# Banded attention beside a memory projection: who splits the weights, and where the scores stand

## Chip, cores and metric
One core of a Trainium2 chip runs the whole program. The metric is the device time of one execution in microseconds (us). The engines are TensorE (PE; its weight loads are PEld), VectorE (DVE), ScalarE (ACT), GpSimd (POOL) and SyncE (SP), which issues most transfers.

## What is computed
One layer of a hybrid decoder for 1024 prompt tokens and 64 sample tokens, 1088 columns in all:

```
x += 0.5 * swiglu_1(norm(x))
h  = norm(x);  u, gate, q, k, v = h @ w_in
     lru_out  = norm(rg_lru(conv(u)) * gelu(gate))
     attn_out = norm(swa(rope(q), rope(k), v))        # blocks of 128 queries over 256 keys, masked to a band, with sinks
x += concat(lru_out, attn_out) @ w_out
mk, mv = norm(mem) @ w_ck, norm(mem) @ w_cv           # 256 memory tokens: the "memory projection"
x += cross_attend(norm(x), mk, mv)
x += 0.5 * swiglu_2(norm(x));  y = norm(x)
```

All values are fp32. Every large product is made of three TensorE products: a weight is split into a high part (rounded to the type fp32r) and a low part (the rest), the activations likewise, and hi*hi + hi*lo + lo*hi is summed.

## The kernel before
Activations lie feature-major, as `[128, tile, 1088]`. The columns are worked in three chunks `CH` of 288, 512 and 288. Each engine has a program of its own, written out by hand and ordered by semaphores.

**Plain projections** (`w_in`, `w_out`, `w_cq`, `w_co`). `plain` (L699) runs tiles of 128 output features, in turn in slot 0 (PSUM banks 0 to 2) and slot 1 (banks 3 to 5). `tile` (L690) has three chunks of 24 matmuls. For `mix` (before `w_in`) and `xattn` (before `w_cq`) the first two tiles run before the norm of their input is known, and `sum_squares` (L565) between tile 0 and tile 1 makes the three column sums of squares with a matmul by ones, into banks 6, 7 and 6 again; `sum_chunk` (L570) waits for VectorE's `mean_squares` (L1288) of the first sum before it writes bank 6 again. On VectorE `mean_squares` handles all three chunks; only then `inverse_rms` (L1297) makes the reciprocal chunk by chunk, and after each chunk `scaled_take` takes that chunk of tile 0 out of PSUM. Tile 2 on TensorE needs tile 0's chunks taken (`g_ev`).

**Banded attention with the memory projection in between.** There are NB = 8 blocks of 128 queries. In a block TensorE runs `block_step` (L822): `scores` of the next block, `turn_p` (transposes of the probabilities) for key head 0, `rotate` for the block after the next, `turn_p` for head 1, `memory_tile` 0, `weigh` 0, `memory_tile` 1, `weigh` 1, `turn_v` of the next block. A `memory_tile` is 24 matmuls of a memory projection, into one place in bank 7. In an even block (s = 0, a pair of `w_ck` tiles) tile 0 reads weight slot 0 and tile 1 slot 1; in an odd block (a pair of `w_cv` tiles) each reads both slots. Each slot has one buffer for the raw weights, one for the high parts and one for the low.

GpSimd splits each slot with `split_short` (L446) in four quarters of 128x256: a multiplication by ones gives the high part (L452), a subtraction the low one (L453). It starts as soon as `mem_mm` says that TensorE is done with the slot. SyncE loads the next raw tile when `w_split` says that the slot is split.

VectorE's `block_step` (L1646) of block b: `add_mask` for b+1 (L1587), `rope_read` (L1572, L1574), `maxima` (L1592 to L1595), `rope` for b+2 (L1579 to L1583), `stage_v`, `take_memory` for both tiles of b (PSUM to SBUF), `probabilities` of b+1 (L1601), `take_result` of b. ScalarE's `block_step` (L1127): two copies of the transposed probabilities (L1131), `exps` of b+1 (L1119, L1121), `take_v` of b+1 (L1125).

After block 6 the sample tokens are rotated, and their scores stand in block 7 between `memory_tile` 0 and `weigh` 0. Behind block 7 ScalarE issues four stores (L1154 to L1159), makes the sample group's exponentials (L1162), VectorE its probabilities (L1684), TensorE turns them (L886, L887) and weighs (L896, L897); then come the squares of the attention's norm (L1003) and the output projection.

Of the kernel before, what the change touches and what calls it, by code (L numbers as in the profile page):

```python
# [22 lines left out]
F32 = mybir.dt.float32  # L23
# [5 lines left out]
P = 128  # L29
# [84 lines left out]
def build(nc, t_in, t_out):  # L114
    ctx = ExitStack()
    with ctx:
        def sem(name):
            return ctx.enter_context(nc.semaphore(name))
# [181 lines left out]
        pt_mm, pt_ev = sem("pt_mm"), sem("pt_ev")  # L300
        v_st, vt_mm, vt_ev = sem("v_st"), sem("vt_mm"), sem("vt_ev")
        pv_mm, o_ev = sem("pv_mm"), sem("o_ev")
        mem_mm, kv_ev = sem("mem_mm"), sem("kv_ev")
        swa_own = sem("swa_own")
        mem_in = sem("mem_in")

# [132 lines left out]
        def _(pool):  # L439
# [45 lines left out]
            def split_plain(s, p):  # L485
                pool.wait_ge(w_in[s], (p + 1) * 16)
                split_short(w_raw[s], w_hi[s], w_lo[s], Steps(pool, w_pool, p * (2 * KT // SHORT) + s * (KT // SHORT)), w_split[s])
# [18 lines left out]
                    .then_inc(lru_normed, 1)  # L506


            for s in range(2):
                pool.wait_ge(mem_mm, 1 + s)  # L510
                split_plain(s, PAIR_KV + 1)
            with pool.Fori(1, NB // 2) as i:
                for s in range(2):
                    pool.wait_ge(mem_mm, i * 4)
                    split_plain(s, i * 2 + PAIR_KV)
                for s in range(2):
                    pool.wait_ge(mem_mm, i * 4 + (1 + s))
                    split_plain(s, i * 2 + (PAIR_KV + 1))
            for s in range(2):
                pool.wait_ge(mem_mm, 2 * NB)  # L520
                split_plain(s, PAIR_OUT)
# [24 lines left out]
        def _(pe):  # L546
# [20 lines left out]
            def sum_squares(key, chunks, adds, src=acc):  # L567

                for c in range(len(chunks)):
                    sum_chunk(key, chunks, c, adds, src)  # L570
# [121 lines left out]
            def tile(stage, p, s, n0, feed=None):  # L692

                pe.wait_ge(w_split[s], p + 1)
                for c, (o, n) in enumerate(CH):
                    pe.wait_ge(g_ev[stage], n0 + c + 1)
                    ins = product(ps[:, 3 * s + c, 0:n], w_hi[s], w_lo[s], c, feed)
                    ins.then_inc(w_mm[s], 1)

            def plain(stage, pair0, pairs, feed, norm=None):  # L700
                tile(stage, pair0, 0, 0, feed=feed)
                if norm:
                    sum_squares(norm, CH, 2 * KT)
                tile(stage, pair0, 1, NC)
                with pe.Fori(1, pairs) as i:
                    for s in range(2):
                        tile(stage, i + pair0, s, i * (2 * NC) + s * NC)
# [90 lines left out]
            def weigh(b, kv):  # L798

                pe.wait_ge(pt_ev, b * 2 + kv + 2)  # L800
                for half in range(2):
                    ins = pe.matmul(ps[kv * HD:(kv + 1) * HD, 6, :], v_n[half][:, kv * HD:(kv + 1) * HD],
                                    p_T[:, half, kv * GRP:(kv + 1) * GRP, :], start=(half == 0), stop=(half == 1))
                return ins
# [16 lines left out]

            def block_step(b, s, more=True, rot=True):  # L822

                if more:
                    scores(b + 1)
                pe.wait_ge(p_done, b + 1)
                turn_p(b, s, 0)
                if rot:
                    rotate(b + 2)
                turn_p(b, s, 1)  # L830
                pe.wait_ge(vt_ev, b + 1)
                if rot:
                    pe.wait_ge(rot_ev, b + 3)
                else:
                    pe.wait_ge(o_ev, b + 1)
                memory_tile(b, s, 0)
                if not more:
                    sample_scores()
                weigh(b, 0)
                memory_tile(b, s, 1)  # L840
                weigh(b, 1).then_inc(pv_mm, 1)
                if more:
                    turn_v(b + 1)

# [27 lines left out]
            rotate(1)  # L872
            pe.wait_ge(rot_ev, 2)
            turn_v(0)
            pe.wait_ge(memn_lo_done, 1)
            with pe.Fori(0, NB // 2 - 1) as i:
                block_step(i * 2, 0)
# [26 lines left out]


            pe.wait_ge(x_tab, 16)
            pe.wait_ge(g_ev["cq"], 6 + NC * KT)

            def x_scores(b):
# [82 lines left out]
        def _(act):  # L992
# [130 lines left out]
            def take_v(b, s):  # L1123
                act.wait_ge(vt_mm, b + 1)
                act.activation(v_n[s][:, :], ps[:, 7, WIN:2 * WIN], ACT.Copy).then_inc(vt_ev, 1)  # L1125

            def block_step(b, s, more=True):  # L1127
                for kv in range(KVH):

                    act.wait_ge(pt_mm, b * 2 + kv + 1)  # L1130
                    act.activation(p_T[:, :, kv * GRP:(kv + 1) * GRP, :], ps[:, 4:6, :], ACT.Copy)\  # L1131
                       .then_inc(pt_ev, 1)
                if more:
                    exps(b + 1, 1 - s)
                    take_v(b + 1, 1 - s)

            act.sem_inc(pt_ev, 1)
            exps(0, 0)
# [40 lines left out]
            for c in range(NC):  # L1179
                hi_parts("cat", cat_tile, "g_cat", lambda c: act.wait_ge(attn_normed, c + 1), [c], range(LT, KT))  # L1180
                if c < NC - 1:
                    hi_parts("cat", cat_tile, "g_cat", chunks=[c + 1], tiles=range(LT))
            act.dma_start(t_out["mem_k"], mem_kT[:, :, :]).then_inc(stored, 16)
            act.dma_start(t_out["mem_v"], mem_v[:, :, :]).then_inc(stored, 16)

# [86 lines left out]
        def _(dve):  # L1272
# [337 lines left out]

            ROPE_STEPS, SWA_STEPS = 1, 5

            def take_memory(b, s, j):

                dve.wait_ge(mem_mm, b * 2 + j + 1)
                if s == 0:
                    to = mem_kT[:, bass.ds(b + j, 1), :].squeeze(1)
                else:
                    to = mem_v[:, j, bass.ds(b * P - P, 2 * P)]
                take_out(to, ps[:, 7, 256:512]).then_inc(kv_ev, 1)  # L1620

            def take_result(b):
# [4 lines left out]
            def block_step(b, s, rot=True):  # L1627
                steps = Steps(dve, swa_own, b * (ROPE_STEPS + SWA_STEPS) + (2 * ROPE_STEPS + SWA_STEPS))
                add_mask(b + 1, 1 - s, masks[:, 2 - s, :])
                if rot:  # L1630
                    rope_read(b + 2)
                maxima(b + 1, 1 - s, steps)
                if rot:
                    rope(b + 2, s, steps)
                stage_v(b + 1)
                for j in range(2):
                    take_memory(b, s, j)
                probabilities(b + 1, 1 - s, steps)
                assert steps.n == SWA_STEPS + (ROPE_STEPS if rot else 0)
                take_result(b)  # L1640
# [26 lines left out]
                              q_r[:, :, 0:TS].rearrange("p g (b t) -> p g b t", b=NS),  # L1667
                              rot_q[:, :, 0:TS].rearrange("p g (b t) -> p g b t", b=NS), ALU.add)
            dve.tensor_tensor(ks_r[:, :], ks_r[:, :], rot_k[:, 0:TS], ALU.add).then_inc(s_rope, 1)
            take_memory(NB - 1, 1, 0)  # L1670
            own.done(dve.tensor_scalar(st8[:, 7, 0:4], c_("sink_s", 0, 4), HD ** 0.5, None, ALU.mult))
            dve.wait_ge(kvc_in, 48)
            dve.wait_ge(s_sc_mm, 1)
# [3 lines left out]
            own.done(dve.tensor_tensor(st8[:, 0, 0:4], st8[:, 0, 0:4], st8[:, 7, 0:4], ALU.max))  # L1677
            own.done(dve.tensor_scalar(st8[:, 1, 0:4], st8[:, 0, 0:4], -(HD ** -0.5), None, ALU.mult))
            dve.tensor_tensor(st8[:, 2, 0:4], st8[:, 1, 0:4], c_("sink_s", 0, 4), ALU.add).then_inc(s_nmax, 1)
            take_memory(NB - 1, 1, 1)  # L1680
            dve.wait_ge(s_exp, 1)
            own.done(dve.tensor_tensor(st8[:, 5, 0:4], st8[:, 3, 0:4], st8[:, 4, 0:4], ALU.add))
            own.done(dve.reciprocal(st8[:, 6, 0:4], st8[:, 5, 0:4]))
# [284 lines left out]
```

## Time and profile before

| | us |
|---|---|
| median of 3 runs | 2483.28 (2482.21 to 2483.57) |
| the profiled execution: its time | 2480.83 |
| its span | 2479.0 |
| PE busy / DVE / POOL / ACT busy in it | 2333.8 / 1431.7 / 1029.9 / 444.1 |
| mean granted TensorE clock | 0.973 of full speed |

The span is what the trace shows from the first to the last instruction; 1.8 us of the execution's time lie outside of it. Busy time of matmuls is modelled, so start times are the surer reading. In the rows below a timeline row has: start in us, length in us, engine, line, operation, written<-read, count, and in square brackets how long the engine had been idle and what ended that. "ACTq" is ScalarE's sequencer while it issues a transfer.

### The profile page before, as it was taken

The page shows a single profiled execution, that of the slowest core. Times are in us where ns is not written, and L with a number is a line of the kernel's source. Part 1 is how long each engine was busy: PE and PEld are TensorE (multiplying, and loading weights), DVE is VectorE, ACT ScalarE, POOL GpSimd, SP SyncE. Part 2 cuts the span into 40 slices and gives each one's busy share as a digit, 9 for nine tenths or more (in the row PEclk, how much of TensorE's full clock was granted, in tenths as well). Part 3 has the DMA queues.
Part 4 walks back from the last instruction along what each step waited for, and adds up shares of the span by engine and source line. Part 5 has one row for each costly group of instructions (what it writes and reads, how often), then busy time and mean ns, then how long its engine had stood idle before and what let it go on. Part 6 is the DMA issues. An engine that isn't in the chain of part 4 may idle for free.

```text
span 2479.0 us, 35690 instructions
## 1 busy us (share of the span) xinstructions
PE 2333.8 (94%) x13994; PEld 2070.5 (84%) x13994; DVE 1431.7 (58%) x1864; ACT 444.1 (18%) x908; POOL 1029.9 (42%) x717
## 2 busy tenths in 40 slices
PE   6999999999999999688789989999999999999997
PEld 5899998999998887556578977889998999999896
DVE  7755555655555775876454324447655655565564
ACT  5111100110110416233322013231000000000002
POOL 2543443434433164546635430344434434344333
PEclk9999999999999999899889999999999999999998
DMA  4111101111010010201211134011011110110102
GB/s 142 69 40 45 47 20 51 51 51 51 34 42 26 26 43 26 97 28 58 71 55 48 34 137 170 26 59 69 21 47 51 51 51 35 50 40 28 68 0 74
DMA packets 40285, 131.89 MB, mean 53 GB/s; under 512 B 5799, under 2 KB 11047, under 8 KB 37799
## 3 DMA queue, kind: packets, MB, share of 16 engines
q1 hardware_dynamic: 37280, 127.80, 14.8%
q10 hardware_dynamic: 2951, 3.35, 0.4%
q8 instruction: 36, 0.59, 0.1%
q14 instruction: 18, 0.15, 0.0%
HBM read 123.33 MB, written 7.81 MB: 53 GB/s over the span
## 4 chain that ended last, share of the span: by engine, by line
PE 85%; DVE 6%; POOL 5%; ACT 3%; issue 1%; DMA 1%; POOLq 0%; SPq 0%; DVEq 0%; ACTq 0%
PE ps L552 27%; PE ps L554 26%; PE ps L553 26%; POOL w_hi L452 2%; POOL w_lo L453 1%; PE ps L961 1%; PE ps L914 1%; DVE act_lo L1315 1%; DVE rstd L1302 1%; DVE mem_raw L1544 1%; PE ps L737 1%; PE ps L578 0%; ACT sq L1003 0%; DVE y L1825 0%; ACT act_hi L1018 0%
## 5 line engine op out<-in xcount | busy, mean ns | idle before, releaser
L552 PE MATMUL ps<-act_hi,w_hi 128*128 128x288 f32 (+1 forms) x1968 | 658.0, 334 | 48.0 <-DVE act_lo L1315 34.8
L553 PE MATMUL ps<-act_lo,w_hi 128*128 128x288 f32 (+1 forms) x1968 | 653.1, 332 | 0.0
L554 PE MATMUL ps<-act_hi,w_lo 128*128 128x288 f32 (+1 forms) x1968 | 652.6, 332 | 0.0
L552 PEld LDWEIGHTS ps<-act_hi,w_hi 128*128 128x128 f32 x1968 | 377.5, 192 | 81.9 <-issue 38.6
L553 PEld LDWEIGHTS ps<-act_lo,w_hi 128*128 128x128 f32 x1968 | 377.6, 192 | 29.6
L554 PEld LDWEIGHTS ps<-act_hi,w_lo 128*128 128x128 f32 x1968 | 377.0, 192 | 29.1
L452 POOL TENSOR_TENSOR w_hi<-w_raw,ones 128x256 fp32r<-128x256 f32 x216 | 193.9, 898 | 472.2 <-PE ps L554 440.0
L1358 DVE SCALAR_TENSOR_TENSOR x<-ps,x 128x288 f32<-128x288 f32 (+1 forms) x504 | 263.6, 533 | 188.0 <-PE ps L554 172.8
L552 PE MATMUL ps<-hid_hi,dn_hi 128*128 128x288 f32 (+1 forms) x1056 | 348.7, 330 | 3.6 <-issue 3.6
L554 PE MATMUL ps<-hid_hi,dn_lo 128*128 128x288 f32 (+1 forms) x1056 | 347.7, 329 | 0.0
L553 PE MATMUL ps<-hid_lo,dn_hi 128*128 128x288 f32 (+1 forms) x1056 | 347.7, 329 | 0.0
L552 PE MATMUL ps<-act_hi,up_hi 128*128 128x288 f32 (+1 forms) x1056 | 347.6, 329 | 0.0
L554 PE MATMUL ps<-act_hi,up_lo 128*128 128x288 f32 (+1 forms) x1056 | 347.5, 329 | 0.0
L553 PE MATMUL ps<-act_lo,up_hi 128*128 128x288 f32 (+1 forms) x1056 | 347.5, 329 | 0.0
L1351 DVE TENSOR_TENSOR hid_lo<-hid_t,hid_hi 128x288 fp32r<-128x288 f32 x132 | 329.7, 2549 | 0.4
L443 POOL TENSOR_TENSOR w_hi<-w_raw,ones 128x1024 fp32r<-128x1024 f32 x42 | 102.0, 2428 | 506.8 <-PE ps L554 490.6
L1326 DVE TENSOR_TENSOR gate_t<-ps,rstd 128x288 f32<-128x288 f32 x132 | 70.0, 532 | 375.7 <-PE ps L554 375.1
L443 POOL TENSOR_TENSOR dn_hi<-w_raw,ones 128x1024 fp32r<-128x1024 f32 x22 | 52.9, 2406 | 396.1 <-PE ps L554 325.2
L552 PEld LDWEIGHTS ps<-hid_hi,dn_hi 128*128 128x128 f32 x1056 | 199.9, 189 | 19.2 <-issue 4.0
L554 PEld LDWEIGHTS ps<-hid_hi,dn_lo 128*128 128x128 f32 x1056 | 199.7, 189 | 16.0
L553 PEld LDWEIGHTS ps<-hid_lo,dn_hi 128*128 128x128 f32 x1056 | 200.0, 189 | 15.3
L553 PEld LDWEIGHTS ps<-act_lo,up_hi 128*128 128x128 f32 x1056 | 198.5, 188 | 16.0
(244 smaller groups left out, 2934.3 us busy)
## 6 DMA issues: line engine op xcount, KB each, us to landing
w_raw<-in_w_ffn SPq DMA_DIRECT2D x66, 512.0 KB, 3.7
w_raw<-in_w_plain SPq DMA_DIRECT2D x54, 512.0 KB, 3.6
ff_raw_up<-in_w_ffn SPq DMA_DIRECT2D x44, 512.0 KB, 4.4
ff_raw_down<-in_w_ffn SPq DMA_DIRECT2D x22, 512.0 KB, 6.4
ck_T<-in_ck SPq DMA_DIRECT2D x8, 1024.0 KB, 7.7
cv_n<-in_cv SPq DMA_DIRECT2D x8, 1024.0 KB, 4.9
x<-in_x SPq DMA_DIRECT2D x2, 1152.0 KB, 11.0
x<-in_x SPq DMA_DIRECT2D x1, 2048.0 KB, 12.0
```

The lines of the kernel that those rows point to most:

```text
L443: steps.done(pool.tensor_tensor(hi[:, :, :], raw[:, :, :], one, ALU.mult))
L452: steps.done(pool.tensor_tensor(hi[:, r, :], raw[:, r, :], one, ALU.mult))
L453: ins = pool.tensor_tensor(lo[:, r, :], raw[:, r, :], hi[:, r, :].bitcast(F32), ALU.subtract)
L552: pe.matmul(out, wh, ah, start=(first and n == 0), stop=False)
L553: pe.matmul(out, wh, al, start=False, stop=False)
L554: ins = pe.matmul(out, wl, ah, start=False, stop=end)
L737: pe.matmul(ps[:, 6 + n_ % 2, 0:n], bd[:, ct, j // NC, :], mix[:, M_U + ct, o:o + n], start=True, stop=True).then_inc(lru_mm, 1)
L914: pe.matmul(ps[:, h // 2, (h % 2) * NM:(h % 2 + 1) * NM], xq_b[:, 2 * h + d, :], mem_kT[:, 2 * h + d, :], start=(d == 0), stop=(d == 1))
L961: ins = pe.matmul(ps[:, 6 + kt // 4, (kt % 4) * P:(kt % 4 + 1) * P], mem_v[:, mt, kt * P:(kt + 1) * P], xp_T[:, mt, kt // 2, :], start=(mt ...
L1326: dve.tensor_tensor(gate_t[:, o:o + n], ps[:, c, 0:n], rstd[:, o:o + n], ALU.mult)\
L1351: dve.tensor_tensor(hid_lo[s][:, o:o + n], hid_t[:, o:o + n], hid_hi[s][:, o:o + n].bitcast(F32), ALU.subtract).then_inc(f["hid_lo"], 1)
L1358: dve.scalar_tensor_tensor(out=x[:, m, o:o + n], in0=ps[:, DOWN_BANKS[n_ % 8], 0:n], scalar=0.5, in1=x[:, m, o:o + n], op0=ALU.mult, op1=A ...
```

## The change
1. **Scores.** `scores` no longer opens a TensorE block. `scores(1)` stands in front of the loop, and a block b with `rot` ends with `weigh` 1, `scores(b+2)`, `turn_v(b+1)`.
2. **High parts.** In the seven blocks 0 to 6 ScalarE copies each whole raw slot (128x1024) to its high part, behind `take_v`; it signals `kv_hi`. GpSimd only subtracts, four quarters a slot.
3. **Takes.** VectorE takes memory tile 0, now in front of `rope`; ScalarE takes memory tile 1, in front of `take_v`, and in block 7 in front of the four stores.
4. **Sums of squares.** In `plain` with a norm the third sum is made behind tile 1 and not in front of it.
5. Two waits on `kv_ev` are added in front of the users of the memory keys and values.

```diff
-            for s in range(2):
-                pool.wait_ge(mem_mm, 1 + s)
-                split_plain(s, PAIR_KV + 1)
-            with pool.Fori(1, NB // 2) as i:
-                for s in range(2):
-                    pool.wait_ge(mem_mm, i * 4)
-                    split_plain(s, i * 2 + PAIR_KV)
-                for s in range(2):
-                    pool.wait_ge(mem_mm, i * 4 + (1 + s))
-                    split_plain(s, i * 2 + (PAIR_KV + 1))
+            with pool.Fori(0, NB - 1) as b:
+                for s in range(2):
+                    pool.wait_ge(kv_hi, b * 2 + (s + 1))
+                    for k in range(0, KT, SHORT):
+                        r = slice(k, k + SHORT)
+                        ins = pool.tensor_tensor(w_lo[s][:, r, :], w_raw[s][:, r, :], w_hi[s][:, r, :].bitcast(F32),
+                                                 ALU.subtract)
+                    ins.then_inc(w_split[s], 1)
+            pool.sem_inc(w_pool, (NB - 1) * (2 * KT // SHORT))
...
                 if norm:
-                    sum_squares(norm, CH, 2 * KT)
+                    sum_squares(norm, CH[:2], 2 * KT)
                 tile(stage, pair0, 1, NC)
+                if norm:
+                    sum_chunk(norm, CH, 2, 2 * KT)
...
             def block_step(b, s, more=True, rot=True):
-                if more:
-                    scores(b + 1)
...
                 weigh(b, 1).then_inc(pv_mm, 1)
+                if rot:
+                    scores(b + 2)
                 if more:
                     turn_v(b + 1)
...
             turn_v(0)
+            scores(1)
...
+            def take_memory(b, s):
+                act.wait_ge(mem_mm, b * 2 + 2)
+                if s == 0:
+                    to = mem_kT[:, bass.ds(b + 1, 1), :].squeeze(1)
+                else:
+                    to = mem_v[:, 1, bass.ds(b * P - P, 2 * P)]
+                act.activation(to, ps[:, 7, 256:512], ACT.Copy).then_inc(kv_ev, 1)
...
                 if more:
                     exps(b + 1, 1 - s)
+                take_memory(b, s)
+                if more:
                     take_v(b + 1, 1 - s)
+                    for j in range(2):
+                        act.wait_ge(w_in[j], b * 16 + (PAIR_KV + 2) * 16)
+                        act.activation(w_hi[j], w_raw[j][:, :, :], ACT.Copy).then_inc(kv_hi, 1)
...
                 maxima(b + 1, 1 - s, steps)
+                take_memory(b, s)
                 if rot:
                     rope(b + 2, s, steps)
                 stage_v(b + 1)
-                for j in range(2):
-                    take_memory(b, s, j)
                 probabilities(b + 1, 1 - s, steps)
...
-            take_memory(NB - 1, 1, 0)
+            take_memory(NB - 1, 1)
...
             dve.tensor_tensor(st8[:, 2, 0:4], st8[:, 1, 0:4], c_("sink_s", 0, 4), ALU.add).then_inc(s_nmax, 1)
-            take_memory(NB - 1, 1, 1)
```

## Rows read from the trace of the kernel before
**Rows 1.** The page's chain that ended last, shares of the span by engine.
```profile
PE 85%; DVE 6%; POOL 5%; ACT 3%; issue 1%; DMA 1%; POOLq 0%; SPq 0%; DVEq 0%; ACTq 0%
```
**Rows 2.** Timeline of TensorE, blocks 4 and 5 (T = 1138.29 and 1156.75).
```profile
1138.29 1.93 PE L802 MATMUL ps<-p_T,v_n 128*64 128x512 f32 x4
1140.16 0.33 PE L788 MATMUL ps<-ident,v_b 128*128 128x128 f32 x1
1140.41 2.00 PE L780 MATMUL ps<-k_r,q_r 64*128 64x256 f32 x16
1142.37 1.09 PE L794 MATMUL ps<-ident,s_m 128*128 128x128 f32 x8
...
1146.68 0.39 PE L552 MATMUL ps<-memn_hi,w_hi 128*128 128x256 f32 x1 [1.02 <-POOL w_lo L453]
...
1153.68 0.39 PE L552 MATMUL ps<-memn_hi,w_hi 128*128 128x256 f32 x1 [2.01 <-POOL w_lo L453]
...
1156.75 1.93 PE L802 MATMUL ps<-p_T,v_n 128*64 128x512 f32 x4
...
1167.73 0.55 PE L552 MATMUL ps<-w_hi,memn_hi 128*128 128x256 f32 x1 [3.64 <-POOL w_lo L453]
```
**Rows 3.** Timeline of GpSimd in the same blocks.
```profile
1138.55 0.73 POOL L452 TENSOR_TENSOR w_hi<-w_raw,ones 128x256 fp32r<-128x256 f32 x1 [10.52 <-PE ps L554]
...
1140.04 2.79 POOL L452 TENSOR_TENSOR w_hi<-w_raw,ones 128x256 fp32r<-128x256 f32 x1
...
1166.90 0.73 POOL L453 TENSOR_TENSOR w_lo<-w_raw,w_hi 128x256 fp32r<-128x256 f32 x1
```
**Rows 4.** Busy us (x instructions) of PE, PEld, DVE, ACT, POOL; PEclk; DMA share; GB/s.
```profile
1128.10:1133.40 5.30, 5.27 (x25) 5.16 (x25) 1.79 (x5) 4.13 (x17) 0.00 (x0) 0.53 0.33 99
```
**Rows 5.** Timeline of TensorE, block 0's memory tile 1.
```profile
1079.34 0.36 PE L552 MATMUL ps<-memn_hi,w_hi 128*128 128x256 f32 x1 [1.47 <-DVE mem_kT L1277]
```
**Rows 6.** Timeline of ScalarE: a copy of 2048 columns; then take_v and 1024 columns.
```profile
1045.43 1.91 ACT L1113 ACTIVATE memn_hi<-mem_raw 128x2048 fp32r<-128x2048 f32 x1 [15.79 <-DVE mem_raw L1544]
...
1140.52 0.28 ACT L1125 ACTIVATE v_n<-ps 128x128 f32<-128x128 f32 x1 [8.29 <-PE ps L788]
1143.49 1.03 ACT L1131 ACTIVATE p_T<-ps 128x1024 f32<-128x1024 f32 x1 [2.70 <-PE ps L794]
```
**Rows 7.** Timelines of TensorE, then of ScalarE, about block 7's end.
```profile
1214.77 1.93 PE L802 MATMUL ps<-p_T,v_n 128*64 128x512 f32 x4
1217.09 0.33 PE L886 MATMUL ps<-ident,ss_m 128*128 128x128 f32 x1 [0.39 <-DVE ss_m L1684]
...
1204.80 0.65 ACTq L1154 DMA_DIRECT2D out_k_sample<-kc_T  x1
...
1208.07 0.32 ACTq L1159 DMA_DIRECT2D out_v_sample<-vs_n  x1
1212.17 0.41 ACT L1162 ACTIVATE ss_m<-ss_m,st 128x136 f32<-128x136 f32 x1 [6.36 <-DVE st L1679]
```
**Rows 8.** Timeline of ScalarE: one store issued in front of a computation.
```profile
1004.75 0.39 ACTq L1104 DMA_DIRECT2D out_small<-small  x1
1005.19 1.94 ACT L1003 ACTIVATE sq<-mix 128x544 f32<-128x544 f32 x3 [7.36 <-DVE mix L1522]
```
**Rows 9.** Timeline of TensorE: the sums of squares of mix, tile 1, tile 2.
```profile
842.11 2.12 PE L578 MATMUL ps<-acc,ones 128*128 128x288 f32 x6 [0.44 <-DVE acc L1286]
843.85 0.51 PE L552 MATMUL ps<-act_hi,w_hi 128*128 128x288 f32 x1
...
856.01 0.29 PE L552 MATMUL ps<-act_hi,w_hi 128*128 128x288 f32 x1
```
**Rows 10.** Timeline of VectorE in the same stretch: the three reciprocals.
```profile
844.73 1.94 DVE L1302 RECIPROCAL rstd<-rstd 128x288 f32<-128x288 f32 x1
...
847.09 3.34 DVE L1302 RECIPROCAL rstd<-rstd 128x512 f32<-128x512 f32 x1
...
851.07 1.94 DVE L1302 RECIPROCAL rstd<-rstd 128x288 f32<-128x288 f32 x1
```

More of the change, by code:

```diff
@@ L302, in build @@
         pv_mm, o_ev = sem("pv_mm"), sem("o_ev")
-        mem_mm, kv_ev = sem("mem_mm"), sem("kv_ev")
+        mem_mm, kv_ev, kv_hi = sem("mem_mm"), sem("kv_ev"), sem("kv_hi")
         swa_own = sem("swa_own")
@@ L906, in _ @@
             pe.wait_ge(x_tab, 16)
+            pe.wait_ge(kv_ev, 2 * NB + 1)
             pe.wait_ge(g_ev["cq"], 6 + NC * KT)
@@ L1182, in _ @@
                     hi_parts("cat", cat_tile, "g_cat", chunks=[c + 1], tiles=range(LT))
+            act.wait_ge(kv_ev, 2 * NB + 1)
             act.dma_start(t_out["mem_k"], mem_kT[:, :, :]).then_inc(stored, 16)
@@ L1611, in _, with take_memory @@
             ROPE_STEPS, SWA_STEPS = 1, 5
-            def take_memory(b, s, j):
-                dve.wait_ge(mem_mm, b * 2 + j + 1)
+            def take_memory(b, s):
+                dve.wait_ge(mem_mm, b * 2 + 1)
                 if s == 0:
-                    to = mem_kT[:, bass.ds(b + j, 1), :].squeeze(1)
+                    to = mem_kT[:, bass.ds(b, 1), :].squeeze(1)
                 else:
-                    to = mem_v[:, j, bass.ds(b * P - P, 2 * P)]
+                    to = mem_v[:, 0, bass.ds(b * P - P, 2 * P)]
                 take_out(to, ps[:, 7, 256:512]).then_inc(kv_ev, 1)
```

## Prediction, made before the changed kernel was run
> **What bounds the kernel now.** I read three views in this order: the page's chain, the timelines around the edited lines, and the busy time by stretch where the clock matters. The chain [rows 1] is TensorE for 85% of the span and GpSimd for 5%, so what the change can give or take lies where TensorE waits. In the banded attention it waits for GpSimd's low parts: 1.02 and 2.01 us in the even block 4, 3.64 us in the odd block 5 [rows 2]. GpSimd starts with the end of a block's last matmul (1138.55) and works without a pause to 1167.63 [rows 3], 29 us for the four slots of two blocks; TensorE adds the two tiles behind it. I measure a block from the start of one second `weigh` to the next, T to T'. Block 4 takes 1156.75 - 1138.29 = 18.5 us [rows 2]. Read the same way blocks 1, 2, 3, 5, 6 and 7 take 16.3, 18.5, 21.1, 20.2, 17.5 and 20.3. In the stretches where the third sum of squares is moved, TensorE does not wait now: from 842.11 three sums take 1.74 us and tile 1 follows at 843.85 [rows 9]; at `xattn` it is much the same.
>
> **Part 1, scores, high parts and takes: the attention blocks.** With T at zero, the new order gives this chain. `weigh` 1 takes 1.87 (1138.29 to 1140.16), scores 1.96 (1140.41 to 1142.37) [rows 2], so `turn_v` starts at 3.83, `take_v` 0.36 later (1140.16 to 1140.52) and ends at 4.47 [rows 2, 6]. Then the two high parts: 1024 columns each, between 0.96 (half of 1.91) and 1.03 [rows 6]; I take 1.0, since the first reads SBUF and writes fp32r as the change does. They end at 5.47 and 6.47. GpSimd subtracts four quarters a slot. A row is 0.73 long [rows 3], four are 2.9; rows without a wait between them overlap a little, so I take 2.8 for a slot: slot 0 is ready at 8.3, slot 1 at 11.1.
>
> What is queued behind the new work: on ScalarE the copy of head 0's probabilities waits for the second high part. In rows 2 and 6 it runs at T+5.2; now it runs from 6.47 to 7.49. TensorE's second `turn_p` waits for it, from 7.55 to 8.5. So an even block starts tile 0 at 8.5 and then has a tile of 3.07 (1153.68 to 1156.75 [rows 2]), 1.87 and 3.07: 16.5 us. An odd block needs both slots: it starts at 11.2 and takes 19.2 at the full clock. TensorE is idle for 2.7 us before that tile. After 3.64 us of idle time, block 3's tile ran at a granted clock of 0.53, the 1.2 GHz level, and took 5.2 us in place of 3.07 [rows 2, 4]; the wait of 2.01 us in block 4 was followed by a tile of 3.07, the 2.4 GHz level [rows 2]. So 19.2 to 21.3; I take 19.7.
>
> VectorE is not late in this: `add_mask` follows the scores at T+4, maxima end near T+10.6, ScalarE's exponentials near T+15, and `probabilities` lie near T', where GpSimd rests. The move of its take in front of `rope` removes the 1.47 us of block 0 [rows 5]. GpSimd's 2.79 us quarter, against 0.73 [rows 3], lies beside VectorE's L1601, the probabilities, and nothing else of that length; that overlap goes, and is already absent in my 2.8.
>
> Sum to the last block: block 0 ends 1.5 earlier, at 1080.9. Three odd blocks at 19.7 and three even at 16.5 give T6 = 1189.5. Block 7: the sample rotation needs `take_result` (T+2.65), the transposed values are copied by ScalarE behind the two high parts (4.5 to 5.5), slot 1 is ready at 9.1; 9.2 + 3.07 + 1.0 (sample scores) + 1.87 + 3.07 = 18.2, so T7 = 1207.7 against 1214.77: 7.1 us earlier, between 2.3 (odd blocks at 21.3) and 8.6 (at 19.2).
>
> **Part 2, what ScalarE's take does behind block 7.** This is where most of that is given back. `take_memory(7)` waits for the last memory tile, and behind it on ScalarE are queued four store issues and the sample exponentials, for which VectorE, TensorE and the whole output projection wait. Now the issues run from 1204.80 to 1208.39, hidden, and the exponentials wait for VectorE until 1212.17 [rows 7]. In the new kernel they start at T7. Whether an issue holds back the computation behind it is shown by one row only: a store took 0.39 and the squares began 0.05 after it [rows 8]. I take them as holding. Then: 3.65 for the issues, 1.8 for the exponentials (1212.17 to 1213.95), 1.82 on VectorE, so TensorE turns the sample's probabilities at T7+7.3, where it now does at 1217.09, T7+2.3 [rows 7]: +5.0. If issues hold nothing it is T7+4.0, +1.7.
> The Trainium skill, "Perfetto Trace Analysis", section "What 'DMA-bound' means", says that a transfer's slice on the issuing engine's sequencer is the making of its descriptors, not data movement. By that rule the engine's next instruction waits for the slice, the 3.6 us count in full (+5.0); read as mere data movement they would not (+1.7). The pair in rows 8 agrees with the rule.
> TensorE is then idle for some 5.4 us (it was 0.39), longer than the wait that ended in 0.53. Its turning and its weighing (1219.34 to 1229.3, of which the first 2.5 us ran at full clock) cost up to 2.3 more; I take +1.8. Part 1 and 2 together: -7.1 + 5.0 + 1.8 = -0.3, between -8.6 + 1.7 = -6.9 and -2.3 + 5.0 + 2.3 = +5.0.
>
> **Part 3, the third sum of squares.** It removes no wait. Its cost: VectorE's `mean_squares` runs over all chunks before the first reciprocal, so it now stands until tile 1 has ended. Tile 1 starts 0.48 earlier, at 843.37, runs 12.15 (843.85 to 856.0) and ends at 855.5; the third sum ends at 856.0. VectorE's mean starts 0.79 after the sum's start and takes 0.46 with the reciprocal behind at 856.73; the first reciprocal and take need 2.36 (844.73 to 847.09 [rows 10]), the take's end and the signal 0.1, and tile 2 starts at 859.2 where it was 856.01 [rows 9]. Its first chunk ends at 862.4, but the second needs another reciprocal and take, 3.98 (847.09 to 851.07), ready at 863.15; chunk 1 started 3.16 into tile 2, at 859.17. So TensorE is 4.0 us late. All that follows starts on this TensorE work, so nothing hides it. The idle time is 3.2 us, between the 2.01 with the full clock behind it [rows 2] and the 3.64 with half [rows 4]; if the clock falls, the first chunk takes 5.8 and the delay is 5.9. I take 5.0. `xattn` has the same order of instructions and the same durations (reciprocals of 1.94 and 3.34, and tile 1 without a wait before it): 5.0 again. Together +10, between 8.0 and 11.8.
>
> **Edits with one answer.** The two waits on `kv_ev` are met long before; `scores(1)` ahead of the loop stands where it ran before; the increment of `w_pool` is one instruction. SyncE's weight loads wait for `w_split`, which now comes 8 or 11 us into a block, and land in 3.6 us, before the next high parts: nothing, unless a load took over 8 us.
>
> **Sum.** -0.3 + 10 = +9.7 us. On the profiled execution (2480.83) that is 2490.5; the median of the runs is 2.45 above that execution, so 2483.28 + 9.7 = 2493.0. The bounds together: +1.1 to +16.8.
>
> **Rivals.**
> *A. The stage keeps its gain, not slower.* Place: ScalarE behind block 7. If the four issues hold nothing back, TensorE idles only 2.1 us there and keeps its clock: -7.1 + 1.7 = -5.4, and with part 3 at 8.0 to 10.0 the total is +2.6 to +4.6, about 2487; with odd blocks at 19.2 down to +1.1. It decides for "no change" where the two parts of the sum differ by less than 5.0. Rows 8 speak against it.
> *B. The change doesn't do what it says.* The high parts come behind `turn_v` and `take_v`, so the subtractions start 5.5 us into a block, where GpSimd now starts at once. If ScalarE is late besides, or GpSimd's quarters meet a VectorE operation with two SBUF inputs in all seven blocks (2.79 - 0.73 = 2.06 each, 14.4 in all [rows 3]), the gain of 7.1 is gone: 2500 to 2507. For it: GpSimd and L1601 did meet in every block. Against: L1601 now falls near T', before the subtractions.
> *C. Half clock everywhere.* Three odd blocks at 21.3 and both gaps of part 3: +11.8 + 5.0, 2500. For it, idle times of 2.7 and 3.2 are near those that were followed by the slow level.
> *D. Faster.* TensorE waits behind both gaps for other work: in the recurrence's gates (2.10, 2.10 and 1.29 us for ScalarE), in the cross attention (4.47 us for ScalarE). If these waits absorb part 3 whole, with A and odd blocks at 19.2 the total is -6.9, 2476. It needs that work to start at an unchanged time; against it, VectorE's convolution starts only on TensorE's tile 3, and the cross attention on the last tile of `w_cq`.
>
> **How the numbers follow.** Forecast (+6 to +14) 0.62; A 0.15; B 0.07; C 0.11; D 0.05. A measurement of this kernel can tell about 0.2% (5 us) from no change. Slower by more: forecast, B, C and a little of A, 0.78; within: 0.17; faster: 0.05. The range leaves out B, D and the ends of A and C: 2484.5 to 2500.
>
> **What would show it.** Right: TensorE idle before tile 2 of `w_in` and of `w_cq` for some 3 us, ended by VectorE's take; blocks of 16.5 (even) and 19 to 20 (odd); GpSimd's quarters at 0.73 without a 2.79; the sample exponentials directly behind four ACTq rows that start with the end of the last memory tile. Wrong: no such gap at tile 2 (part 3 falls, and the kernel is no slower), or even blocks over 18 us (B), or exponentials running beside the ACTq rows (A).

## The result and the profile after

The changed kernel is slower, and by more than I had said.

| | before | after |
|---|---|---|
| median (4 runs of each, on one chip) | 2482.74 | 2500.68 (2497.77 to 2501.79) |
| ratio, 95% interval | | 1.0072 (1.0054 to 1.0089) |
| the profiled execution: time / span | 2480.83 / 2479.0 | 2501.79 / 2500.0 |
| mean granted clock | 0.973 | 0.966 |

That is +17.9 us in medians, where I had forecast +9.7 (2493.0, between 2484.5 and 2500.0). The two profiled executions are 21.0 apart: the one of after lies 1.1 above its median, the one of before 1.9 below, so 3 of the 21 are differences between runs.

The page of after, busy time and the chain by engine:

```profile
PE 2348.5 (94%) x13994; PEld 2083.5 (83%) x13994; DVE 1423.5 (57%) x1856; ACT 460.1 (18%) x930; POOL 971.5 (39%) x661
...
PE 88%; DVE 6%; ACT 3%; issue 1%; POOL 1%; DMA 0%; ACTq 0%; SPq 0%; DVEq 0%; POOLq 0%
```

GpSimd lost 58 us of work (1029.9 to 971.5) and fell from 5% of the chain to 1% [rows 1], so the change does what it says. The kernel didn't gain by it: TensorE's busy time rose by 15 us, with the same products to make. What TensorE waited for between 600 and 1500 us (total, times, longest; "issue" is a wait for which the profile shows no cause):

```profile
PE ps L551 <- issue: 14.1, 6, 3.7
PE ps L795 <- ACT p_T L1142: 9.2, 7, 2.3
...
PE ps L888 <- DVE ss_m L1699: 4.8, 1, 4.8
...
PE ps L551 <- DVE mix L1429: 2.9, 1, 2.9
PE ps L551 <- DVE xq L1429: 2.9, 1, 2.9
```

Before, one line stood here for GpSimd's low parts, 17.5 us in ten waits. Four things took its place: odd blocks' wait for the low parts (now under "issue", which stood at 6.0 us in three waits before: three more of 2.7), the second `turn_p` behind ScalarE's copy, the sample's turn, and the two tiles 2 of part 3. To see where the time is lost I read the start of the same instruction in both profiled executions. Tn is the start of block n's second `weigh`, and block n runs from the T before it to Tn:

| instruction | before | after | late by | expected |
|---|---|---|---|---|
| sums of squares of `mix` | 842.11 | 842.63 | 0.5 | 0 |
| first convolution, VectorE | 880.89 | 886.12 | 5.2 | 5.0 |
| first `rotate` (after the gates) | 1046.83 | 1054.31 | 7.5 | 5.0 |
| second `weigh` of block 7 (T7) | 1214.77 | 1220.63 | 5.9 | -2.1 |
| sample's result copied, VectorE | 1229.32 | 1241.84 | 12.5 | 4.7 |
| first tile of `xattn` | 1356.81 | 1371.25 | 14.4 | 4.7 |
| first scores of the cross attention | 1458.79 | 1477.94 | 19.2 | 9.7 |
| second feed-forward layer | 1660.25 | 1681.16 | 20.9 | 9.7 |

The tail and part 3 came as I had said: +6.7 from T7 to the sample's result (I had +6.8), and +4.7 in each of the two projections (I had 5.0). The attention's blocks gave 1.6 us where I had 7.1. And three stretches that the change doesn't touch became longer: the gates by 2.3, the output projection by 1.9, the cross attention by 1.8.

Part 3 in after: TensorE's tile 2 of `w_in`, VectorE in front of it, and the same tile of `w_cq`:

```profile
859.56 0.40 PE L551 MATMUL ps<-act_hi,w_hi 128*128 128x288 f32 x1 [2.90 <-DVE mix L1429]
...
856.70 0.46 DVE L1311 TENSOR_SCALAR rstd<-ps 128x288 f32<-128x288 f32 x1 [11.73 <-PE ps L577]
857.08 1.94 DVE L1319 RECIPROCAL rstd<-rstd 128x288 f32<-128x288 f32 x1
859.05 0.46 DVE L1429 TENSOR_TENSOR mix<-ps,rstd 128x288 f32<-128x288 f32 x1
859.43 3.34 DVE L1319 RECIPROCAL rstd<-rstd 128x512 f32<-128x512 f32 x1
...
1402.63 0.40 PE L551 MATMUL ps<-act_hi,w_hi 128*128 128x288 f32 x1 [2.90 <-DVE xq L1429]
```

VectorE stands for 11.73 us until the third sum is there, and then the reciprocals of [rows 10] follow while TensorE waits 2.90.

The odd block 5 and the start of block 6 in after, TensorE, then ScalarE and GpSimd of block 5:

```profile
1161.97 1.93 PE L803 MATMUL ps<-p_T,v_n 128*64 128x512 f32 x4
...
1169.26 1.09 PE L795 MATMUL ps<-ident,s_m 128*128 128x128 f32 x8 [1.15 <-ACT p_T L1142]
1173.05 0.55 PE L551 MATMUL ps<-w_hi,memn_hi 128*128 128x256 f32 x1 [2.70 <-issue]
...
1190.61 1.09 PE L795 MATMUL ps<-ident,s_m 128*128 128x128 f32 x8 [2.30 <-ACT p_T L1142]
...
1162.18 0.38 ACT L1136 ACTIVATE mem_kT<-ps 128x256 f32 x1 [1.26 <-PE ps L553]
1166.12 0.28 ACT L1128 ACTIVATE v_n<-ps 128x128 f32<-128x128 f32 x1 [3.56 <-PE ps L789]
1166.29 2.00 ACT L1151 ACTIVATE w_hi<-w_raw 128x1024 fp32r<-128x1024 f32 x2
1168.19 1.01 ACT L1142 ACTIVATE p_T<-ps 128x1024 f32<-128x1024 f32 x1
...
1167.42 5.53 POOL L514 TENSOR_TENSOR w_lo<-w_raw,w_hi 128x256 fp32r<-128x256 f32 x8 [10.71 <-ACT w_hi L1151]
```

The chain is the predicted one: T (here T4) is 1161.97, ScalarE takes the values and makes two high parts, GpSimd's eight quarters take 5.53 (2.8 a slot), and the tile starts at T+11.1 (I had 11.2). In windows (busy us of PE, PEld, DVE, ACT, POOL; PEclk; DMA share; GB/s), tile 2 of `w_in`, block 5's tile 0, and blocks 0 to 5:

```profile
859.50:862.80 3.30, 3.24 (x18) 3.24 (x19) 3.27 (x2) 0.00 (x0) 2.61 (x4) 0.71 0.00 0
...
1173.00:1178.40 5.40, 5.35 (x24) 5.19 (x24) 0.00 (x0) 4.14 (x17) 0.00 (x0) 0.51 0.36 112
...
1088.00:1183.00 95.00, 81.16 (x468) 58.91 (x467) 63.65 (x86) 43.17 (x115) 27.74 (x40) 0.93 0.19 55
```

Block 5's tile took 5.4 us at a clock of 0.51, the 1.2 GHz level, behind an idle time of 2.7 us. The odd blocks 1, 3 and 5 took 20.5, 20.5 and 21.4 us, the even blocks 2 and 4 took 16.3, blocks 6 and 7 took 18.0 and 19.3: 132.3 us from T0 to T7, where before took 132.4.

The end of the attention in after, ScalarE and then TensorE:

```profile
1220.74 0.38 ACT L1136 ACTIVATE mem_v<-ps 128x256 f32<-128x256 f32 x1 [8.65 <-PE ps L553]
1220.74 0.65 ACTq L1170 DMA_DIRECT2D out_k_sample<-kc_T  x1
1221.43 0.68 ACTq L1171 DMA_DIRECT2D out_k_sample<-ks_r  x1
1222.14 1.56 ACTq L1173 DMA_DIRECT2D out_v_sample<-v_c  x1
1223.74 0.28 ACTq L1175 DMA_DIRECT2D out_v_sample<-vs_n  x1
1224.07 0.41 ACT L1178 ACTIVATE ss_m<-ss_m,st 128x136 f32<-128x136 f32 x1 [2.95 <-issue]
...
1227.41 0.48 PE L888 MATMUL ps<-ident,ss_m 128*128 128x128 f32 x1 [4.85 <-DVE ss_m L1699]
```

The four issues follow one another for 3.3 us (I had 3.65), the exponentials start 0.05 behind the last, and the turn comes at T7+6.8 (I had T7+7.3).

### The profile page after: what moved, and what is told of

Read it like the earlier page. It is cut to its first block, busy times and chain, and to the rows that moved or that the text cites. A ratio compares the mean times of both kernels' runs of the same rounds, so it can differ in the third digit from the quotient of the medians.

```text
span 2500.0 us, 35600 instructions
## 1 busy us (share of the span) xinstructions
PE 2348.5 (94%) x13994; PEld 2083.5 (83%) x13994; DVE 1423.5 (57%) x1856; ACT 460.1 (18%) x930; POOL 971.5 (39%) x661
## 3 DMA queue, kind: packets, MB, share of 16 engines
q1 hardware_dynamic: 37280, 127.80, 14.7%
## 4 chain that ended last, share of the span: by engine, by line
PE 88%; DVE 6%; ACT 3%; issue 1%; POOL 1%; DMA 0%; ACTq 0%; SPq 0%; DVEq 0%; POOLq 0%
PE ps L551 27%; PE ps L552 27%; PE ps L553 27%; PE ps L917 1%; PE ps L803 1%; PE ps L964 1%; DVE act_lo L1332 1%; DVE rstd L1319 1%; PE ps L781 1%; PE ps L738 1%; DVE mem_raw L1561 1%; PE ps L577 1%; PE ps L795 0%; ACT sq L1006 0%; DVE y L1840 0%
## 5 line engine op out<-in xcount | busy, mean ns | idle before, releaser
L452 POOL TENSOR_TENSOR w_hi<-w_raw,ones 128x256 fp32r<-128x256 f32 x160 | 136.8, 855 | 436.4 <-PE ps L553 404.4
L551 PEld LDWEIGHTS ps<-hid_hi,dn_hi 128*128 128x128 f32 x1056 | 200.0, 189 | 19.3 <-issue 4.0
L551 PEld LDWEIGHTS ps<-act_hi,up_hi 128*128 128x128 f32 x1056 | 198.5, 188 | 16.1
## 6 DMA issues: line engine op xcount, KB each, us to landing
x<-in_x SPq DMA_DIRECT2D x2, 1152.0 KB, 10.9
```

What stands on the lines that cost most here:

```text
L452: steps.done(pool.tensor_tensor(hi[:, r, :], raw[:, r, :], one, ALU.mult))
L551: pe.matmul(out, wh, ah, start=(first and n == 0), stop=False)
```

## Experiments

### Part 3 by itself, and its idle time filled

`sum_only` is the kernel before with part 4 of the change; nothing else is touched.

```diff
                 if norm:
-                    sum_squares(norm, CH, 2 * KT)
+                    sum_squares(norm, CH[:2], 2 * KT)
                 tile(stage, pair0, 1, NC)
+                if norm:
+                    sum_chunk(norm, CH, 2, 2 * KT)
```

> The kernel before with part 4 of the change alone: the third sum of squares behind tile 1. Theory: tile 2 of w_in and of w_cq starts some 3 us late behind VectorE's reciprocal and its second chunk once more, 4.0 to 4.7 us for each of the two stages, +8 to +9.5 us in all, and up to 3 more if the gates of the recurrence run at the lower clock level, as they did in the changed kernel. Rival (the extra loss in the gates and in the cross attention is chance or belongs to the attention blocks): +8 to +9.5 and gates as before. Rival (the gap is absorbed by later waits): within 2 us of the kernel before.

Measured: 2493.58, ratio 1.0043 (1.0029 to 1.0056), +11.1 us. Both gaps are there:

```profile
860.21 0.40 PE L552 MATMUL ps<-act_hi,w_hi 128*128 128x288 f32 x1 [2.90 <-DVE mix L1414]
...
1396.38 0.40 PE L552 MATMUL ps<-act_hi,w_hi 128*128 128x288 f32 x1 [2.90 <-DVE xq L1414]
```

The stretch from the sums to the convolution takes 43.47 (before 38.78), that from `xattn` to the cross attention 106.71 (101.98): 4.7 each. The gates are longer here too (168.2, before 165.9).

`sum_filled` adds to `sum_only` twenty matmuls behind the third sum, into a bank that is free there.

```diff
+                    pe.wait_ge(ssq_ev, SUM0[norm] + 2)
+                    for _n in range(20):
+                        pe.matmul(ps[:, 7, 0:288], act_hi[:, 0, 0:P], act_hi[:, 0, 0:288], start=True, stop=True)
```

> The kernel before with part 4, and 20 further matmuls of 288 columns on bank 7 behind the third sum, where TensorE is idle for 2.9 us. They compute nothing that is used. Theory (VectorE's reciprocals cost 4.0 us in each stage, and the rest of the 11 us is the lower clock level behind the idle time): tile 2 still starts 3 us late, but its matmuls of 288 columns are 0.13 us apart from the start; the delay of each stage is 4.0 and not 4.7 us; 1 to 3 us less than with part 4 alone. Rival (the clock plays no part there): the same time as with part 4 alone.

Measured: 2489.24, ratio 1.003 (1.0018 to 1.0041), 4.3 below `sum_only`, more than the 1 to 3 expected. Timeline of TensorE, and then the window of tile 2's first 3.3 us:

```profile
856.37 3.01 PE L709 MATMUL ps<-act_hi 128*128 128x288 f32 x20
859.65 0.40 PE L552 MATMUL ps<-act_hi,w_hi 128*128 128x288 f32 x1 [0.27 <-DVE mix L1417]
```

```profile
859.50:862.80 3.30, 3.15 (x24) 3.15 (x24) 3.30 (x2) 0.00 (x0) 2.78 (x4) 1.00 0.00 0
```

The tile starts no later (17.0 behind the first sum, 16.9 in `sum_only`) and runs at 1.00 in place of after's 0.71 in the same place. The two stretches are now longer than before's by 3.96 and 4.04: this is the waiting for VectorE alone, and what is above it, 0.7 each, is the clock. These two explain 1.4 of the 4.3 us; the rest lies in stretches between (below). Two runs described below agree. In `late_take` the second gap of 2.90 was not followed by the lower level (1.00 over the tile's first 3.3 us), and the stretch is 3.96 longer than in `both_back`, which has no gap. In `filled` the level was low from the tile's start behind the first gap (0.50), and the stretch is 5.9 longer than before's.

### Part 3 and the tail undone

`sum_back` is after without part 4. `late_take` is after with ScalarE's take of block 7 behind the sample's exponentials. `both_back` has both.

```diff
-                take_memory(b, s)
                 if more:
+                    take_memory(b, s)
                     take_v(b + 1, 1 - s)
...
             act.activation(st8[:, 3, 0:4], st8[:, 2, 0:4], ACT.Exp).then_inc(s_exp, 1)
+            take_memory(NB - 1, 1)
```

> The changed kernel with part 4 undone. Theory: 8 to 12 us less than the changed kernel, so +6 to +10 against the kernel before, what is left being the end of the attention (ScalarE's take in front of four store issues) less the 1.5 us of block 0. Rival (the sums are harmless and the attention blocks carry the loss): at most 3 us less than the changed kernel.

> The changed kernel with ScalarE's take of block 7's last memory tile moved behind the sample group's exponentials. Theory: the four store issues are again hidden in block 7, the exponentials start when VectorE has the maxima, TensorE turns the sample's probabilities 2 us behind the last tile and not 6.8, and its 33 small products start at the full clock: 6 to 7 us less than the changed kernel. Rival (the stores' issue is not what holds the exponentials, or the squares wait for the stores' landing): less than 2 us.

> The changed kernel with part 4 undone and ScalarE's take of block 7 behind the sample group's exponentials: scores, high parts and takes of the blocks remain. Theory: the two costly edits are gone and with them some 18 of the 18 us; the blocks themselves give 1.5 us (block 0) and lose what they gain to the lower clock level, so the time is that of the kernel before within 3 us: 2480 to 2485. Rival (the two corrections overlap, or the blocks carry a loss of their own): 2486 or more.

Measured: `sum_back` 2488.88, ratio 1.0024 (1.0014 to 1.0034), 11.8 below after. `late_take` 2489.91, 1.0032 (1.0022 to 1.0043), 10.8 below after, where 6 to 7 were expected. `both_back` 2480.93, 0.9999 (0.999 to 1.0008), 19.8 below after. The end of block 7 in `late_take`:

```profile
1216.51 1.93 PE L803 MATMUL ps<-p_T,v_n 128*64 128x512 f32 x4
1218.37 0.33 PE L888 MATMUL ps<-ident,ss_m 128*128 128x128 f32 x1
```

The turn follows `weigh` at once, and from T7 to the sample's result `late_take` takes 14.7 us; after took 21.2, before 14.55. So the tail costs 6.5 in place; the rest of the 10.8 lies elsewhere. With both undone the kernel is as before: the rest of the change, which I had counted at -7.1, is worth 1.1 us, and the interval reaches from 2.5 us gained to 2.0 lost. In its profile block 0 ends 1.5 us earlier, and T0 to T7 takes 132.2 us, as in after and in before.

### The blocks: is it the clock?

`filled` is after with twenty matmuls (`FILL` is 20) in the odd blocks, in front of the wait for the low parts, into the place that the tile then overwrites.

```diff
-                for slot in ((j,) if s == 0 else (0, 1)):
-                    pe.wait_ge(w_split[slot], b + (PAIR_KV + 1))
                 pe.wait_ge(kv_ev, b * 2 + j + 1)
                 out = ps[:, 7, 256:512]
+                if s == 1 and j == 0:
+                    for _n in range(FILL):
+                        pe.matmul(out, memn_hi[:, 0, 0:P], memn_hi[:, 0, :], start=True, stop=True)
+                for slot in ((j,) if s == 0 else (0, 1)):
+                    pe.wait_ge(w_split[slot], b + (PAIR_KV + 1))
```

> The changed kernel with 20 further matmuls of 256 columns on the place in bank 7 that memory tile 0 of an odd block then starts anew; they stand in front of its wait for the weights, where TensorE is idle for 2.7 us. They compute nothing that is used. Theory (the odd blocks take 20.5 to 21.4 us and not 19.2 because the tile behind the wait runs at the lower clock level, and the level hangs on the idle time): the tiles of blocks 1, 3 and 5 take 3.1 us in place of 4.5 to 5.4, odd blocks 19.1 to 19.5, 4 to 6 us less than the changed kernel. Rival (the clock falls for another reason, or the level would be held only by much more work): tiles still over 4 us, time the same within 2 us.

Measured: 2495.28, ratio 1.0046 (1.0033 to 1.006), 5.4 below after. Block 1's tile, and its first 3.1 us:

```profile
1100.05 0.36 PE L552 MATMUL ps<-w_hi,memn_hi 128*128 128x256 f32 x1 [0.40 <-POOL w_lo L515]
```

```profile
1099.50:1102.60 3.10, 2.70 (x23) 2.58 (x22) 0.43 (x1) 2.64 (x11) 0.41 (x1) 1.00 0.68 209
```

The odd blocks take 19.1 each (I had worked out 19.2 for the full clock), and T0 to T7 takes 127.5 in place of 132.3. The wait for GpSimd ends when it did; only the clock behind it differs. Of the 5.5 us that were missing in the blocks, 4.7 came back: 5.0 in the odd blocks and 0.4 in block 6, less 0.7 in block 7.

### The blocks: is it the place of the high parts?

`hi_first` is after with the two copies in front of `take_v`, so that they don't wait for TensorE to turn the values.

```diff
                 if more:
-                    take_v(b + 1, 1 - s)
                     for j in range(2):
                         act.wait_ge(w_in[j], b * 16 + (PAIR_KV + 2) * 16)
                         act.activation(w_hi[j], w_raw[j][:, :, :], ACT.Copy).then_inc(kv_hi, 1)
+                    take_v(b + 1, 1 - s)
```

> The changed kernel with the two high parts in front of ScalarE's take_v in each block, so that they don't wait for TensorE's scores and turn_v. Theory (the place behind take_v is what keeps the blocks as long as before): high parts start 0.5 us into a block and not 4.4, the slots are ready at 4.5 and 7.2, TensorE no longer waits for them, every block falls to 15 to 16 us and the clock stays at the upper level; T0 to T7 takes 110 to 115 us in place of 132, so 15 to 22 us less than the changed kernel. Rival (VectorE or the loads of raw weights become the bound): blocks over 17.5 us, 5 to 10 us less.

Measured: 2475.50, ratio 0.9972 (0.9963 to 0.9981), 25.2 below after, more than the 15 to 22 expected. Block 2, TensorE, ScalarE and GpSimd:

```profile
1101.60 1.93 PE L803 MATMUL ps<-p_T,v_n 128*64 128x512 f32 x4
...
1109.02 0.36 PE L551 MATMUL ps<-memn_hi,w_hi 128*128 128x256 f32 x1 [0.23 <-DVE rot_k L1591]
...
1101.81 0.38 ACT L1136 ACTIVATE mem_v<-ps 128x256 f32 x1 [1.44 <-PE ps L553]
1102.09 1.99 ACT L1150 ACTIVATE w_hi<-w_raw 128x1024 fp32r<-128x1024 f32 x2
1105.75 0.28 ACT L1128 ACTIVATE v_n<-ps 128x128 f32<-128x128 f32 x1 [1.66 <-PE ps L789]
1106.62 1.02 ACT L1142 ACTIVATE p_T<-ps 128x1024 f32<-128x1024 f32 x1 [0.59 <-PE ps L795]
...
1103.22 5.55 POOL L514 TENSOR_TENSOR w_lo<-w_raw,w_hi 128x256 fp32r<-128x256 f32 x8 [9.85 <-ACT w_hi L1150]
```

```profile
1086.00:1163.00 77.00, 75.85 (x468) 53.81 (x466) 57.52 (x86) 43.75 (x115) 27.74 (x40) 1.00 0.23 68
```

The copies start at T+0.5 and not at T+4.3, GpSimd is done at T+7.2, and that is when TensorE has its transposes behind it. Five blocks take 15.4 us each, odd and even alike, block 6 takes 14.9 and block 7 17.6: T0 to T7 is 109.5 in place of 132.3. The clock is 1.00 through all of it, where after had 0.93. So the 3.8 us by which the copies started later in each block decided over the whole stage. Of the 22.8 us, three odd blocks lost 3.7 each at the full clock (19.1 - 15.4) and 1.7 each by the lower one (20.8 - 19.1), two even blocks 0.9 each (for the copy of the probabilities), block 6 lost 3.1 and block 7 1.7.

### The scores' new place, and the version that is left

`scores_only` is before with part 1's order of the scores alone. `best` is after with the high parts first, part 4 undone and the late take. `scores_back` is `best` with the old place of the scores.

```diff
-                if more:
-                    scores(b + 1)
                 pe.wait_ge(p_done, b + 1)
...
                 weigh(b, 1).then_inc(pv_mm, 1)
+                if rot:
+                    scores(b + 2)
...
             turn_v(0)
+            scores(1)
```

> The kernel before with part 1's order of the scores alone: scores(b+2) and then turn_v at a block's end. Theory (GpSimd's splits bind the blocks, not the scores): blocks take the 16.3 to 21.2 us of the kernel before, the time is the same within 3 us; at most VectorE's probabilities move against GpSimd's quarters and a 2.8 us quarter goes. Rival (the scores ahead shorten the blocks by themselves): 5 us or more less than the kernel before.

> The kernel with high parts in front of take_v, part 4 undone and the last take behind the sample's exponentials. Theory: the sum of the three, 2463 to 2469, faster than the kernel before by 14 to 20 us. Rival (the raw weights' loads or VectorE bound the blocks): 2475 to 2481.

> The best kernel so far (high parts in front of take_v, the sums and the last take put back) with the scores where the kernel before has them, at a block's start. Theory (with the splits out of the way TensorE's own work is the bound, and VectorE's mask, maxima and the exponentials of the next block only just fit): scores ahead matter now, blocks of 16.5 to 18 us without them, 8 to 15 us more than the best kernel. Rival (the order of the scores does nothing in either kernel): within 3 us of the best kernel, blocks of 15.4.

Measured: `scores_only` 2481.18, ratio 0.9998 (0.9988 to 1.0007). `best` 2457.82, 0.991 (0.9895 to 0.9926), 24.2 us below before; 2463 to 2469 had been expected, so it lies 5 us below the lower bound. `scores_back` 2459.49, 0.9912 (0.9898 to 0.9925). The place of the scores does nothing to the times that is clear of the spread between runs, in either kernel; on TensorE's chain the same instructions stand one after the other in both orders. The profiles are not identical: T0 to T7 takes 111.6 in `scores_back` and 109.5 in `best`, 1.5 of it in block 7, where the waits are the same and the clock is 0.91 in place of 1.00; and `scores_only` ends block 0 1.9 later than before, in part with eight transposes of 1.97 us that took 1.09. Whether the order of the scores moves the clock there, or the execution does, is not shown. What is worth having of the change is that two engines share the split, provided that the first of them starts at once.

## Why the prediction was right and wrong

Right, by its own steps. Part 3: the gap stands where I put it, ended by VectorE's take, and costs 4.0 by waiting and 4.7 with the clock (I had 4.0 and 5.0). My bounds of 4.0 and 5.9 were both met, the one in `late_take` and the other in `filled`, by where the clock fell. The tail: issues hold back the computation behind them, +6.7 for +6.8. The closeness is luck: the turn came 4.5 later than in before where I had 5.0, and what follows it cost 2.2 where I had 1.8. The block's chain: tile 0 at T+11.1 (11.2) in an odd block, T+8.5 (8.5) in block 6, even blocks of 16.3 (16.5), and block 0 ended 1.5 earlier against the first `rotate` (T0 - 34.0 in place of T0 - 35.6). The 2.79 us quarter [rows 3] is gone in after: eight quarters take 5.53, and none of them meets VectorE's probabilities (L1601 before). The Trainium skill, "SBUF — State Buffer", section "SBUF: two separate sides", says that GpSimd and a VectorE operation with two SBUF inputs lock each other out of a shared port pair for a whole instruction; the trace agrees, 2.79 us with such an operation beside it and 0.73 without; beside VectorE operations with one input in PSUM (L1604, L1589) the quarters of after took 0.72 to 0.74.

Wrong, first term: "19.2 to 21.3; I take 19.7" for an odd block. The wait was right; what the clock costs behind it was sized too small. The bounds held for the mean (20.5, 20.5 and 21.4, mean 20.8), the value between them was taken at the wrong end. I had two rows, 2.01 us of idle time with the full clock behind it and 3.64 with the half, and put 2.7 near the first. `filled` shows that it belonged to the second. For block 6 I had seen TensorE's wait for the second `turn_p`, but not that the clock would fall behind it (2.30 us idle, no `rotate` to cover it): 18.0 in place of 16.5. Block 7 took 19.3 in place of 18.2; it takes 17.6 in `best`, at a clock of 1.00. That makes 3 x 1.1 + 1.5 + 1.1 = 5.9, less 0.4 for two even blocks: 5.5 of the missing 11.3 us.

Wrong, second term: there was none for the stretches that the change doesn't touch. Between the profiled executions the gates are 2.3 us longer, the output projection 1.9, the cross attention 1.8, 5.9 in all. The clock is part of it: the first score matmuls of the cross attention, before and then after, wait 1.90 both times, and then take 3.69 or 5.38 us.

```profile
1458.79 3.69 PE L914 MATMUL ps<-mem_kT,xq_b 128*128 128x256 f32 x16 [1.90 <-DMA x_id<-in_ident]
```

```profile
1477.94 5.38 PE L917 MATMUL ps<-mem_kT,xq_b 128*128 128x256 f32 x16 [1.90 <-DMA x_id<-in_ident]
```

Which of the two a kernel gets is not settled. Up to the next wait this stretch takes 9.2 to 9.4 us in before, `sum_back`, `both_back`, `late_take`, `sum_filled` and `scores_only`, and 10.9 in after, `sum_only`, `filled`, `hi_first`, `best` and `scores_back`; the clock over its first 9.2 us is 0.98 in before and 0.81 in after. A gap of part 3 in front of it doesn't decide it: `late_take` has the gap and the short stretch, `best` has no gap and the long one.

The gates are ordered by the clock too. Their first 145 us in before, after and `late_take`:

```profile
880.90:1025.90 145.00, 138.64 (x752) 116.41 (x751) 109.32 (x133) 59.87 (x66) 73.66 (x79) 0.98 0.13 41
```

```profile
886.10:1031.10 145.00, 137.56 (x739) 115.17 (x738) 107.62 (x134) 59.84 (x66) 72.58 (x79) 0.96 0.13 41
```

```profile
885.60:1030.60 145.00, 138.47 (x762) 116.98 (x761) 110.37 (x134) 59.73 (x66) 73.75 (x80) 0.99 0.13 41
```

With one short stretch at the 1.2 GHz level in there the gates take 164.6 and 165.5 (`late_take`, `scores_only`), with two 165.9 to 167.0 (before, `both_back`, `sum_back`, `sum_filled`, `hi_first`, `best`), with three 168.2 to 168.3 (after, `sum_only`, `filled`, `scores_back`). The output projection takes 129.4 in after and `sum_back`, and 127.5 to 127.9 in all others. So that untouched stretches differ by up to 4 us is shown, and for the gates and the cross attention that the lower level goes with the longer time. What decides it is not shown, and not even that it is the edit upstream: each kernel was profiled once, the sums of squares of `mix`, which stand in front of every edit, start at 841.7 to 843.6 in the twelve profiles, and the unchanged kernel's own runs reach from 2478.0 to 2486.1. So the 4.3 us of `late_take`'s 10.8 and the 2.9 of `sum_filled`'s 4.3 that don't lie at the edited place can't be put down to the edit with any certainty.

The whole sum: 9.7 forecast, 5.5 in the blocks, 5.9 in untouched stretches, 0.5 in front of the first edited line, less 0.7 (my 0.3 too much in each projection and 0.1 in the tail), gives 20.9 of the 21.0 of the profiled pair; 3.0 of it is where these two lie among their runs, and 17.9 is left in medians. The edited places alone make 9.7 + 5.5 - 0.7 = 14.5, which my range would have held and which the interval of the medians (13.4 to 22.1 us) holds too; the 3.4 us beyond it have no cause that a run shows. The range ended at rival C, half clock everywhere, 2500. C was right about the level and on the whole too high about its size (blocks at 21.3, projections at 5.9; each came once, in block 5 and behind `filled`'s first gap), and it had no untouched stretch either; that it gave nearly the measured time is chance. Rival A fell with the ACTq rows, B's overlap with L1601 didn't come, and nothing absorbed part 3, so D fell. B's first half, that the place of the high parts takes the gain, was the true one in a wider sense than I gave it: I had it in my chain as given and didn't price the alternative, which `hi_first` puts at 23 us in the stage.

## To carry to other kernels

When work is moved to a second engine, ask what stands in front of it in that engine's order: here two copies that waited behind an unrelated transpose cost 23 us, about what the mended version gains (24). In a kernel like this one, price an idle time of TensorE of 2.2 to 3.0 us as one that is followed by the 1.2 GHz level (66 of 70 were, by the count below), and put work without dependences into it as an experiment before you believe the sum. And let a range for a kernel with a wandering clock reach some microseconds past the worst case of the edit itself, since stretches that nobody touched differ from profile to profile too.

## What the runs showed of the hardware

- The lower clock came behind shorter idle times than I had thought: 2.70 (block 5, 0.51), 2.30 (block 6's second turn, 18.0 us for the block), 2.90 (tile 2, 0.71 over its first 3.3 us). Of the last the timeline shows that it doesn't come with the idle time itself: the tile's first matmuls start 0.13 us apart, full pitch, and only 1.3 us later 0.24 apart. Which idle times are followed by it can't be told from their length alone: the 1.90 in front of the cross attention's scores stands in all twelve kernels, and the lower level came within 1.3 us behind it in six. Counted over the twelve profiles, where the clock was full when the idle time began: of 70 idle times of 2.2 to 3.0 us, 66 had the lower level begin in them or within 4 us behind them, of 80 of 1.8 to 2.2 us, 45.
- Twenty idle-time matmuls that compute nothing were worth 5.4 us in one kernel (4.7 in the blocks where they stand) and 4.3 in another (1.4 in place). The Trainium skill, "TensorE: Matmul & The Clock Gate", section "HAM oscillation — how this bites in real kernels", describes bursts of matmuls between waits, each of which starts at the slow level again. Block 5 agrees (0.51 over the whole tile); in blocks 1 and 3 the tile's first 0.4 and 1.1 us ran at 1.00 and only then at 0.50. The odd blocks took 20.8 us on average, 19.1 once filled.
- A copy of 1024 columns from fp32 to fp32r takes ScalarE 1.0 us. GpSimd subtracts 128x256 in 0.73 us when it is left alone, and a row of eight takes 0.69 us each.
- ScalarE's sequencer takes 0.28 to 1.56 us to issue one store of these shapes, and the next computation starts 0.05 us after the last. ScalarE's take of 0.38 us ran beside the first of them: both start at 1220.74.
